# Router fed from x ahead of its norm, weight slots reordered, and an expert scatter in four products of 128 rows

## The reference, cut to what matters

```python
for l in range(2):
    mix = hybrid_mixer(x, w_in[l], ...)          # two attentions (8 heads each, 256 rows), then @ w_o
    x = layer_norm(ALPHA * x + mix, ln1_g[l], ln1_b[l])
    ffn = grouped_moe(x, router_w, router_bias, w_gate[l], w_up[l], w_down[l])
    x = layer_norm(ALPHA * x + ffn, ln2_g[l], ln2_b[l])

def layer_norm(x, g, b):
    mu, var = mean(x), mean(square(x - mu))
    return (x - mu) * rsqrt(var + 1e-5) * g + b

def grouped_moe(xt, router_w, router_bias, w_gate, w_up, w_down):   # 16 experts, 4 groups of 4
    aff = sigmoid(xt @ router_w)                 # 256 x 16
    ...                                          # best group by its two best, then 2 experts in it
    gates = one_hot(e_idx) weighted by aff / sum
    hg, hu = xt @ w_gate[e], xt @ w_up[e]        # 1024 x 512 per expert
    out = sum over e of (silu(hg) * hu * gates[e]) @ w_down[e]      # 512 x 1024
```

## Time and profile before

| | |
|---|---|
| three runs | 1147.83, 1144.57, 1147.25 us (median 1147.25) |
| the profiled execution | 1144.47 us, of which its trace spans 1142.7 us |
| mean granted clock of PE | 0.98 of full speed |
| layer 0: attention 1 starts, attention 2 ends | 444.93, 499.65 us |
| layer 0: gather, expert loop, next layer | 528.30, 532.24, about 750 us |

### The profile page before, as it was taken

One profiled execution on the slowest core, in us unless ns is written; L12 is line 12 of the kernel. 1 busy time (PEld: TensorE's weight loads), 2 busy tenths in 40 slices (PEclk: granted clock), 3 DMA queues, 4 the chain that ended last, 5 costly groups with the idle time before them and its releaser, 6 DMA issues.

```text
span 1142.7 us, 16069 instructions
## 1 busy us (share of the span) xinstructions
PE 1082.2 (95%) x6194; PEld 739.6 (65%) x6194; DVE 562.1 (49%) x1060; ACT 421.1 (37%) x755; POOL 90.0 (8%) x115
## 2 busy tenths in 40 slices
PE   7999998999999999898999999989989999999995
PEld 5898988999998797675344443358867634444332
DVE  4764376767667557756222222274784722222224
ACT  5345454555455346633111111143573311111111
POOL 2200000000000012510000000011252000000000
PEclk9999999999999998999999999999989999999998
DMA  8743255564564443349999999943241999999993
GB/s 288 270 148 113 75 175 175 171 201 164 193 207 159 131 132 111 112 165 389 420 421 419 420 420 420 417 158 119 85 171 42 392 390 419 420 420 420 419 420 122
DMA packets 81684, 294.56 MB, mean 258 GB/s; under 512 B 7252, under 2 KB 40386, under 8 KB 56914
## 3 DMA queue, kind: packets, MB, share of 16 engines
q1 hardware_dynamic: 79456, 289.29, 66.2%
q10 hardware_dynamic: 1394, 2.18, 0.5%
q0 software_dynamic: 768, 2.19, 0.5%
HBM read 292.59 MB, written 1.05 MB: 257 GB/s over the span
## 4 chain that ended last, share of the span: by engine, by line
PE 78%; DVE 9%; DMA 5%; ACT 4%; issue 3%; POOL 0%; SPq 0%; DVEq 0%; ACTq 0%
PE bank L2330 16%; PE bank L2339 9%; PE bank L1880 7%; PE bank L1881 7%; PE bank L1882 7%; DMA k_t<-in_w_up 5%; PE bank L1941 4%; PE bank L1943 4%; PE bank L1942 4%; PE bank L1805 4%; PE bank L2317 3%; PE bank L2362 3%; PE bank L1975 2%; PE bank L1959 2%; PE bank L2063 1%
## 5 line engine op out<-in xcount | busy, mean ns | idle before, releaser
L1107 DVE TENSOR_TENSOR lo<-raw,hi 128x2048 fp32r<-128x2048 f32 (+3 forms) x78 | 166.9, 2146 | 62.9 <-ACT hi L695 62.6
L695 ACT CAST hi<-raw 128x2048 fp32r<-128x2048 f32 (+3 forms) x78 | 139.5, 1796 | 60.0 <-PE bank L1882 57.7
L1336 DVE TENSOR_TENSOR proj<-bank,proj 64x512 f32<-64x512 f32 x32 | 34.6, 1082 | 204.5 <-PE bank L2352 192.0
L1941 PE MATMUL bank<-xs,hi 128*128 128x256 f32 x448 | 128.4, 287 | 3.6 <-DVE xs L1137 1.5
L1880 PE MATMUL bank<-hi,xs 128*128 128x512 f32 (+2 forms) x312 | 125.1, 401 | 6.4 <-DVE xs L1141 3.4
L1943 PE MATMUL bank<-xs,lo 128*128 128x256 f32 x448 | 127.5, 285 | 0.0
L1942 PE MATMUL bank<-xs,hi 128*128 128x256 f32 x448 | 127.4, 284 | 0.0
L1881 PE MATMUL bank<-hi,xs 128*128 128x512 f32 (+2 forms) x312 | 119.2, 382 | 0.0
L1882 PE MATMUL bank<-lo,xs 128*128 128x512 f32 (+2 forms) x312 | 118.9, 381 | 0.0
L1045 ACT ACTIVATE proj<-bank 64x512 f32<-64x512 f32 x32 | 18.8, 589 | 202.8 <-PE bank L2331 202.8
L1941 PEld LDWEIGHTS bank<-xs,hi 128*128 128x128 f32 x448 | 86.7, 193 | 5.0 <-issue 3.5
(11 more groups left out here) (286 smaller groups left out, 2096.7 us busy)
## 6 DMA issues: line engine op xcount, KB each, us to landing
raw<-in_w_up SPq DMA_DIRECT2D x40, 1024.0 KB, 5.2
raw<-in_w_in SPq DMA_DIRECT2D x28, 1024.0 KB, 5.3
moe_w<-in_w_gate SPq DMA_DIRECT2D x24, 1024.0 KB, 15.9
moe_w<-in_w_up SPq DMA_DIRECT2D x24, 1024.0 KB, 17.4
moe_w<-in_w_down SPq DMA_DIRECT2D x24, 1024.0 KB, 16.2
raw<-in_w_down SPq DMA_DIRECT2D x19, 1024.0 KB, 5.1
raw<-in_w_gate SPq DMA_DIRECT2D x10, 1024.0 KB, 12.9
raw<-in_w_o SPq DMA_DIRECT2D x8, 1024.0 KB, 4.9
```

What stands on the lines that cost most here:

```text
L695: nc.scalar.copy(high(n)[:, 0:size], raw[:, n % RING, 0:size]).then_inc(S["hi_done"], 1)
L1107: tt(low(n)[:, 0:size], raw[:, n % RING, 0:size], high(n)[:, 0:size].bitcast(F32), ALU.subtract).then_inc(S["lo_done"], 1)
L1941: mm(dst, wh[:, k, col], x_hi, start=k == 0, stop=False)
```

## The change

Three things are changed in both layers.

The router works on x before its norm. With m the row's mean and r its inverse deviation, the logits of layer_norm(x) are r·(x·(g∘W)) − r·m·sum(g∘W) + sum(b∘W). PE transposes the raw sum alpha·x + mix (`turn_x`; of half 0 inside the out products of half 1), makes 16 products of 16 columns in plain fp32 with `router_gb` (`router_products`) in place of the 16 products of 256 columns and the two folding ones, and DVE puts mean, deviation and sums together (`logits_normed`). POOL makes g∘W and b∘W (`router_gb`), and PE sums their columns in 8 products of 32 columns (`gain_sums`) just before attention 1, which an ACT copy takes out ahead of attention 1's exponentials. x itself is normed without gain and shift; these are applied where the gathered rows leave the accumulator (two instructions for one on ACT and DVE), the rows with gain are written back to x by four new DVE instructions (`kept`), and alpha times the shift enters the accumulators by four products of one row. 3 of the fillers stay where 15 were.

The slots of the slabs 4 to 15 are in another order: `attention_slot` and `proj` take slabs 4 and 5 and wait for the end of attention 2 (`weighted`); `wide_a` takes slab 15 and waits for `ln_scaled`, which the last `kept` sets.

The scatter is 4 products of 128 rows: high and low part of an expert's output lie under each other, and ACT and DVE write them in two instructions each, of 64 partitions.

```diff
+        ring_slots = [moe_w[:, RING * part + i, :] for i in (2, 0, 1) for part in range(2)]
         moe_slots = [wide_b[:]] + [raw[:, i, :] for i in range(RING)]
...
+        moe_slots += [attention_slot[:], flat[:, 2 * FFE:2 * FFE + SLAB]] + ring_slots[0:2]
+        moe_slots += [xn[:].rearrange("p a n -> p (a n)")] + ring_slots[2:]
+        moe_slots += [q_t[:].rearrange("p h t -> p (h t)"), k_t[:].rearrange("p h t -> p (h t)"), wide_a[:]]
+        RAW_SLOT, ATTENTION_SLOT, FIRST_RING, XN_SLOT, RING_SLOT, QK_SLOT, GAIN_SLOT = 1, 1 + RING, 6, 8, 9, 13, 15
...
-                    elif m < RING_SLOT:
+                    elif m < ATTENTION_SLOT:
                         sp.wait_ge(S["lo_done"], b + L_O + 1 + m)
+                    elif m < FIRST_RING:
+                        sp.wait_ge(S["weighted"], 2 * HEADS * (2 * layer + 3))
                     elif m < XN_SLOT:
-                        sp.wait_ge(S["slab_used"], b + L_O + 1 + (m - RING_SLOT) // 2)
-                    elif m < MOE_SLOTS - 1:
-                        sp.wait_ge(S["ln_done"], 2 * HALVES * layer + HALVES)
-                    elif m < MOE_SLOTS:
-                        sp.wait_ge(S["router_logits"], layer + 1)
+                        sp.wait_ge(S["slab_used"], b + L_O + 1)
+                    elif m == XN_SLOT:
+                        sp.wait_ge(S["heads_turned"], 4 * (layer + 1))
+                    elif m < QK_SLOT:
+                        sp.wait_ge(S["slab_used"], b + L_O + 2 + (m - RING_SLOT) // 2)
+                    elif m < GAIN_SLOT:
+                        sp.wait_ge(S["slab_used"], b + L_O + 4)
+                    elif m == GAIN_SLOT:
+                        sp.wait_ge(S["ln_scaled"], 2 * HALVES * layer + HALVES)
...
+                for g in range(2):
+                    nc.gpsimd.tensor_tensor(router_gb[:, g], router_w[:],
+                                            columns[:, layer, 0, g, :].unsqueeze(2).broadcast_to([P, DC, EXPERTS]), ALU.mult)
...
+                w.next("gain_sums")
+                nc.scalar.copy(route[:, 4, :], bank[6][:, sums_at])
                 attention(after=lambda i: split_quarter(b + L_O + (i - 4) // 4, (i - 4) % 4) if 4 <= i < 16 else None)
...
+                squares_beside(0, 0)
+                squares_beside(0, 1)
                 heads_high(3)
...
-                centred_squares(0)
+                for c in range(2):
+                    turned_even(0, c)
+                    centred(0, c)
                 wait_slab(act, "slab_used", b + L_O + 1)
                 rows_high(0)
...
+                squares_beside(1, 0)
+                turned_even(1, 0)
+                squares_beside(1, 1)
+                turned_even(1, 1)
+                centred(1, 0)
+                w.next("logits_normed", 2)
+                nc.scalar.activation(route[:, 0, :], route[:, 5, :], ACT.Exp, scale=-1.0).then_inc(S["router_exp"], 1)
+                centred(1, 1)
                 rows_high(1)
...
                 w.next("chosen")
                 nc.vector.tensor_scalar(route[:, 4, :], picked[:], -ELSEWHERE, ELSEWHERE, ALU.mult, ALU.add)\
-                    .then_inc(S["router_step"], 1)
-                w.next("router_step")
+                    .then_inc(S["vector_step"], 1)
+                rows_lo(1, 0)
+                w.next("vector_step")
...
+            def rows_lo(half, i):
+
+                w.next("rows_hi")
+                nc.vector.scalar_tensor_tensor(out=row_chunks(1, half, i), in0=x_chunks(half, i), scalar=stat[:, 2, half:half + 1],
+                                               in1=row_chunks(0, half, i).bitcast(F32), op0=ALU.mult, op1=ALU.subtract)\
+                    .then_inc(S["rows_lo"], 1)
+
+            def kept(half):
+
+                for c in range(2):
+                    part = slice(512 * c, 512 * (c + 1))
+                    ins = nc.vector.scalar_tensor_tensor(out=x[:, half, part], in0=x[:, half, part], in1=ln_gb[:, 0, part],
+                                                         scalar=stat[:, 2, half:half + 1], op0=ALU.mult, op1=ALU.mult)
+                ins.then_inc(S["ln_scaled"], 1)
...
+                def out_low(at, c):
+
+                    rows_ = high_rows[c]
+                    return nc.vector.scalar_tensor_tensor(out=expert_out[low_rows[c], c, :], in0=bank[2][rows_, :],
+                                                          scalar=slot_gate[rows_, at:at + 1],
+                                                          in1=expert_out[rows_, c, :].bitcast(F32),
                                                           op0=ALU.mult, op1=ALU.subtract)
 
...
                 slots_of(0)
+                rows_lo(1, 1)
                 rounds_needed()
...
                 gated_slots(0)
+                w.next("ln_in", 32)
+                for half in range(HALVES):
+                    kept(half)
                 for e in range(EXPERTS):
...
+                column_added(0, 0)
+                column_added(0, 1)
+                variance(0)
+                heads_low(3)
+                turned_odd(0, 0)
+                turned_odd(0, 1)
+                w.next("rstd_ready")
+                rows_lo(0, 0)
+                column_added(1, 0)
+                rows_lo(0, 1)
+                column_added(1, 1)
+                turned_odd(1, 0)
+                variance(1)
+                turned_odd(1, 1)
+                logits_normed(0)
+                w.next("rstd_ready")
+                logits_normed(1)
...
+                for k in range(DC):
+                    ins = mm(bank[6][:, sums_at].rearrange("p (g e) -> p g e", g=2), const[:, C_ONE:C_ONE + 1].broadcast_to([P, P]),
+                             router_gb[:, :, k, :], start=k == 0, stop=k == DC - 1)
+                ins.then_inc(S["gain_sums"], 1)
...
+                def turn_x(half, c):
+
+                    pe.wait_ge(S["ln_added"], 8 * layer + 2 * half + c + 1)
+                    for k in range(4 * c, 4 * c + 4):
+                        ins = turn(bank[2 + k // 2][:, SEQ * half + (k % 2) * P:SEQ * half + (k % 2 + 1) * P], x[:, half, k * P:(k + 1) * P])
+                        if k % 2:
+                            ins.then_inc(S["x_turned"], 1)
+
                 def out_groups(half, first, end):
 
                     for g in range(first, end):
+                        if half and g == DC + 1:
+                            turn_x(0, 0)
+                            turn_x(0, 1)
...
-                busy(15, bank[2])
...
-                for k in range(DC):
-                    fm_chunk(k)
-                    for part in range(2):
-                        ins = mm(bank[0][:, 0:SEQ], router_s[:, k, :], xr[:, k, part * SEQ:(part + 1) * SEQ],
-                                 start=k == 0 and part == 0, stop=k == DC - 1 and part == 1)
-                ins.then_inc(S["router_parts"], 1)
-                w.next("parts_copied")
+                def router_products(half, c):
+
+                    for k in range(4 * c, 4 * c + 4):
+                        if k % 2 == 0:
+                            w.next("x_turned_odd" if k % 4 else "x_turned_even")
+                        ins = mm(bank[6 + half][:, 0:EXPERTS], x_t[:, k, half * P:(half + 1) * P],
+                                 router_gb[:, 0, k, :], start=k == 0, stop=k == DC - 1)
+                    if c:
+                        ins.then_inc(S["router_logits"], 1)
+
...
+                turn_x(1, 0)
+                turn_x(1, 1)
+                router_products(0, 0)
+                router_products(0, 1)
+                router_products(1, 0)
+                router_products(1, 1)
+                busy(3, bank[2])
+                pe.wait_ge(S["ln_in"], 16 * (4 * layer + 2))
+                pe.wait_ge(S["logits_normed"], HALVES * (layer + 1))
                 for half in range(HALVES):
-                    ins = mm(bank[1][:, EXPERTS * half:EXPERTS * (half + 1)], logit_parts[:, half * P:(half + 1) * P],
-                             const[0:2 * EXPERTS, C_FOLD:C_KEPT], start=True, stop=True)
-                ins.then_inc(S["router_logits"], 1)
-                open_acc()
+                    for c in range(2):
+                        mm(acc[half][c][:], const[0:1, C_ALPHA:C_ALPHA + 1].broadcast_to([1, P]),
+                           ln_gb[0:1, 1, 512 * c:512 * (c + 1)], start=True, stop=False)
                 busy(11, bank[2])
...
-                def add_out(at):
+                def add_out(at, c):
 
                     for half in range(HALVES):
-                        for split_ in range(2):
-                            for c in range(2):
-                                part = slice(SLOTS * c, SLOTS * (c + 1))
-                                ins = mm(acc[half][c][:], slot_to_token[part, at, half * P:(half + 1) * P],
-                                         expert_out[part, split_, :], start=False, stop=False)
```

(2 more changed lines are left out.)

332 lines of the change are left out of this document (193 added, 139 removed).

## The result

The changed kernel takes 1164.56 us (four runs, 1163.95 to 1166.18), the one before 1146.79 us; the ratio is 1.0162, with a 95% interval of 1.0143 to 1.0181 (these two medians alone give 1.0155). That is 17.8 us slower, inside the forecast range, 3.6 us above the forecast. The profiled execution of the changed kernel took 1166.18 us with a span of 1164.0, 21.3 us more than the span before; it is that kernel's longest run, and the profiled one of before is its shortest, so the trace shows some 4 us more than the medians.

The account below looks back on a forecast made before the run. Loads bound the expert stage, little ahead of PE. Attention 1.5, gather's end 1.7 and slab 15 3.6 make 6.8 us a layer, 13.6 for two; with ends +0.35, +14.0: 1158.5 on the profiled run, 1161 on the median, range 1156 to 1166.

Parts of the forecast that it names:

- Bound: Expert stage: loads set the end by little; PE at 13.48 us a step eats its store over 80 slabs, 20 us.
- Slots: Slab 15 is issued 4.75 us after the gather, queue dry from about 529: costs 3.6 us a layer.
- Router: Router stage: records 0.12 to 0.13 us each, choices start 2.4 us earlier, gather ends 1.3 us earlier if clock held.
- Rival B: Router's products nearly free: 32 records in 0.8 us, per layer +0.7 us, total 1149 us; chance 0.09.
- Clock: Router stage: PE's clock falls at about 518, costing 3.0 us; gather ends 1.7 us later, not 1.3 earlier.
- the four one-row products and the fillers ahead of the counts 1.4: Between router and gather: these cost 1.4 us more at the fallen clock, part of the 3.0 us.
- Attention: Gain sums ahead of attention 1 and ACT's later table load delay the whole attention 1.5 us a layer (bounds 1.0, 2.2).
- Scatter: Expert loop: 0.2 us less per expert, 6.4 us of PE, hidden by loads; sign: wait for slab 91 grows several us.
- The end of the chain: Layer ends: +0.75 us once for DVE's second low-part instruction, −0.4 for the last scatters, together +0.35.
- A: PE's clock holds in the router stage: 3.8 us a layer, with the ends +8, total 1155 us; chance 0.24.
- C: The load queue never runs dry, loads end 2.6 us earlier in each layer: about −5, 1142 us; chance 0.13.
- D: Clock stays low through the gather or first raise: 1.5 to 3 us more a layer, 1166 or above; chance 0.04.

Follow-up runs that it names:

- half_loads: The kernel before, loading only the first half of each slab from slab 16 on, so its output is not the layer's; 1141.22 us, one run.
- both: Changed kernel with own buffer for gain and shift, slab 15 freed early and the one-row shift products moved into the expert loop; 1155.77 us, 1.0087.
- shift_pool: `both` with the shift added to x by GpSimd, four opening products on zeros instead of one-row products, fewer fillers; 1149.61 us, 1.0031.

## Why the prediction was right, and where it was not

**Bound.** Right: loads lead PE by little. Taking them away gives 1.5 and 2.1 us a layer (`half_loads`), a slot more gives 1.4 and 2.0. The sum behind it was short: it let PE eat the store at 13.48 us a step to the end, but the last four steps have no gather and take 12.19 us, so the store goes some 5 us faster than the 20 us of the forecast.

**Slots.** Slab 15 was issued 4.28 us after the gather's end (forecast 4.75), and the queue was dry from about 529.5 (forecast 529). The sum's 3.6 us a layer measured: 8.3 us later landing less 5.4 us later gather, 2.9 in layer 0; layer 1 has 2.4. Freed early the slab gives 1.5, not 3.1: slab 16 goes out no earlier, and a second hole opens behind the first.

**Router.** The last sum, the transposes and the products' pace came out as walked through: 32 records in 3.64 us, 0.114 each. The chain starts at 520.53, against a forecast of 520.8 with the clock held and of 522.4 with the fall. Rival B, nearly free products, is out.

**Clock.** The fall came, at about 519.6 instead of 518, when the 32 records were through. So one part of its price never came: the second half of the products was to cost 1.6 us more and cost nothing, and the records did not grow to over 0.2 us. The other part is the term that was mis-sized: "the four one-row products and the fillers ahead of the counts 1.4" more. They took 7.19 and 4.87 us, and the counts came 8.4 us behind the choice of experts. The forecast names no row for the one-row products. The nearest of their kind were the gain rows at the layer's end, in the kernel before:

```profile
748.59 1.99 PE L2456 MATMUL bank<-value,const 1*128 1x512 f32 x8
```

These are eight records in 1.99 us, and the changed kernel's gain rows take the same. The shift's records take 0.43 us each at full clock (`both`) and 0.89 at half. The gain rows lie on two partitions (0 and 32), two products on each; the shift row lies on one. That products on two such partitions run beside each other is my reading, no run tested it. And the fillers, meant to fill a wait, were in front of the counts. An estimate from these rows, with 0.22 us a filler (14 in 3.22 us at 759.65): even at full clock the eight records and eleven fillers behind 520.8 would end at about 526.6, some 2.5 us after the choice at 524.1. The other 6 us are the clock. So the end of the gather in layer 0, against attention 2, moved by +5.4 where +1.7 was forecast.

**Attention.** Forecast +1.5 a layer, measured 0.3 at the end of attention 2 in layer 0. The sums took 1.87 us, the table load came behind the copy, and the first attention product came at 446.37:

```profile
444.66 1.87 PE L2361 MATMUL bank<-router_gb,const 128*128 128x32 f32 x16
446.37 0.69 PE L2103 MATMUL bank<-k_t,q_t 128*128 128x128 f32 x4
446.57 0.19 ACT L1032 COPY route<-bank 128x32 f32<-128x32 f32 x1 [1.56 <-PE bank L2361]
446.76 1.28 ACT L820 ACT_TABLE_LOAD   x1
```

That is 1.44 us later than the earlier trace rows, but attention 2 ended only 0.3 later in layer 0, where the kernel before had a stretch at half clock inside attention 1 and this one none; in layer 1, where both had one, the way from norm 2 to the end of attention 2 is 1.7 us longer, of which another stretch at half clock behind the norm may be a part. So the term was there at the start of attention 1. That the clock covered it in layer 0 is the likely reading; no run shows it alone.

**Scatter.** That its 0.2 us an expert would not show was right, but the sign named for it did not come: PE's last wait for a slab grew from 1.12 to 1.33 us only, and three earlier waits of 0.39, 1.33 and 0.81 us are new. The reason given, that the loads hide them, is only half of it: `half_loads` shows that nothing is left even without loads to wait for. The end of the chain was +0.75 − 0.4 in the forecast; alone the scatter costs 1.8 and 1.3 us a layer, in the changed kernel the way from the last slab waited for to the norm grew by 1.4 and 0.6 us.

**Sum.** In the two stretches 5.5 us a layer were forecast (1.7, 3.6 and the ends), 9.2 are there: over both layers the gather's end was 3.8 too small, slab 15 0.9 too large, the end of the chain 0.8 too small. Of the rivals A needed a clock that holds, and C a gather that ends before 528.7; it ended at 538.0. D needed a clock still low in the gather; it was back at 533.2, before the gather's start at 534.16.

The direction and the two mechanisms, the hole ahead of slab 15 and the fall of the clock, were forecast. That the median came within 3.6 us is in part luck. Between the two traces that the sum was made for, 21.3 us were measured and 14 forecast; a term of 1.6 us a layer that never came and an attention term too large stand against one that was several times too small; and the profiled run of before was its kernel's fastest, that of the changed kernel its slowest.

## What to carry to other kernels

When one engine's chain is made shorter, read what stands in the other engines' queues ahead of the meeting point: fillers and set-up products that were hidden under the old chain become the chain. Price a product by a row with the same shape and the same partitions, and a stretch of narrow or one-row products at both clock levels. A load that waits for the last reader of its buffer holds up all behind it in a common queue, so spare memory that makes one slot more comes first.

## What was not expected of the hardware

- One-row plain fp32 products lowered PE's clock to 0.50 for 6.8 us in the middle of a loop that otherwise ran at 1.00 (`both`, 8 records in 4.27 us, in both layers), and it does not fall there without them (`shift_pool`). PE was busy for the whole of the stretch in which it fell (4.00 of 4.00 us).
- An instruction of 512 columns on 64 partitions cost what one on 128 costs: two of them 1.53 us on DVE against 0.75, and 1.39 against 0.69 on ACT.
- With their inputs ready, four scatter products of 128 rows by 512 columns took 0.92 us and eight of 64 rows 1.12 us, so a product of half the rows took more than half the time.
- The same kernel's runs lie up to 12 us apart (`shift_pool`, 1143.83 to 1156.22), and profiles of different runs have their half-clock stretches at different places.
